# Spatial gating's four rounds, each moved one projection tile later

## What is computed

```
h = rms_norm(x, g);  z = h @ w_in
u_a, v_a = gelu(z[:, 0:512]), gelu(z[:, 512:1024])
q, k, v, f = the next 512, 512, 512 and 8 columns
vn = (v_a - mean) * rsqrt(var + eps) * ln_g          # per head of 64
mixed = w_s (masked, 128 x 128 per head) @ vn + b_s  # along a block of 128 positions
out_a = u_a * mixed
out_b = forgetting_attention(q, k, v, f)
x = x + concat(out_a, out_b) @ w_out
```

## Time and profile before

| | |
|---|---|
| median of 3 runs | 3130.44 us (3128.32 to 3130.82) |
| the profiled execution's own time | 3129.38 us |
| its span in the trace | 3127.3 us |
| TensorE busy with matmuls | 2930.7 us, 94% |
| VectorE busy | 1695.3 us, 54% |
| ScalarE busy | 984.3 us, 31% |
| GpSimd busy | 1028.5 us, 33% |
| mean DMA rate | 82 GB/s |

### The profile page before, as it was taken

How to read it: one execution, slowest core, us unless ns; L and a number is a source line. 1 busy time by engine, 2 the same in 40 slices (tenths; PEclk the granted TensorE clock), 3 DMA queues, 4 the chain that set the end, 5 groups by cost and what they waited for, 6 DMA issues and landing times. The chain is left out here.

```text
span 3127.3 us, 43902 instructions
## 1 busy us (share of the span) xinstructions
PE 2930.7 (94%) x16484; PEld 2419.3 (77%) x16484; DVE 1695.3 (54%) x2479; ACT 984.3 (31%) x1741; POOL 1028.5 (33%) x642
## 2 busy tenths in 40 slices
PE   7989899999999999899999989888889799999998
PEld 6768787778888888778878878878778577777776
DVE  5734353764554554555567348788842652067753
ACT  4021461311111111321111127677730201177731
POOL 2433313654445554422222212223243222211231
PEclk9989999999999999999999999999999899999998
DMA  5544521111111111023344321212011132432111
GB/s 182 182 137 136 136 62 47 54 54 47 47 40 47 47 54 40 20 102 113 125 168 148 114 104 43 102 52 94 18 40 37 54 132 76 127 99 51 28 41 68
DMA packets 214183, 255.72 MB, mean 82 GB/s; under 512 B 9401, under 2 KB 182782, under 8 KB 214030
## 3 DMA queue, kind: packets, MB, share of 16 engines
q1 hardware_dynamic: 198450, 190.20, 20.0%
q10 hardware_dynamic: 15584, 63.51, 5.1%
HBM read 188.08 MB, written 65.60 MB: 81 GB/s over the span
## 5 line engine op out<-in xcount | busy, mean ns | idle before, releaser
L1036 PE MATMUL ps<-hh,w_parts 128*128 128x512 f32 (+2 forms) x2560 | 999.8, 391 | 46.3 <-POOL w_parts L816 27.5
L1037 PE MATMUL ps<-hl,w_parts 128*128 128x512 f32 (+2 forms) x2560 | 984.3, 384 | 0.0
L1038 PE MATMUL ps<-hh,w_parts 128*128 128x512 f32 (+2 forms) x2560 | 981.4, 383 | 0.0
L1036 PEld LDWEIGHTS ps<-hh,w_parts 128*128 128x128 f32 x2560 | 488.9, 191 | 157.2 <-issue 37.4
L814 POOL TENSOR_TENSOR w_parts<-w_raw,zero 128x1024 fp32r<-128x1024 f32 x140 | 294.6, 2104 | 956.7 <-PE ps L1038 769.3
L1037 PEld LDWEIGHTS ps<-hl,w_parts 128*128 128x128 f32 x2560 | 490.6, 192 | 104.9 <-issue 5.7
L1038 PEld LDWEIGHTS ps<-hh,w_parts 128*128 128x128 f32 x2560 | 489.5, 191 | 99.9
L816 POOL TENSOR_TENSOR w_parts<-w_raw,w_parts 128x1024 fp32r<-128x1024 f32 x140 | 338.5, 2418 | 11.0
L1977 ACT ACTIVATE f_y<-f_z,convv 128x1024 f32<-128x1024 f32 x44 | 54.8, 1245 | 515.1 <-DVE f_z L2548 514.9
L2548 DVE TENSOR_TENSOR f_z<-ps,f_rs 128x1024 f32<-128x1024 f32 x44 | 53.8, 1223 | 182.9 <-PE ps L1038 182.7
L2750 DVE TENSOR_SCALAR_CACHE_REDUCE b_s<-ps 128x640 f32<-128x640 f32 (+1 forms) x128 | 99.9, 781 | 96.3 <-PE ps L1610 96.2
(11 more groups left out here) (355 smaller groups left out, 4799.3 us busy)
## 6 DMA issues: line engine op xcount, KB each, us to landing
w_mod_sb<-in_w_mod SPq DMA_DIRECT2D x16, 1536.0 KB, 6.9
w_raw<-in_w_up SPq DMA_DIRECT2D x44, 512.0 KB, 3.7
w_raw<-in_a_w_in SPq DMA_DIRECT2D x32, 512.0 KB, 4.4
d_raw<-in_w_down SPq DMA_DIRECT2D x22, 512.0 KB, 4.1
w_raw<-in_w_in SPq DMA_DIRECT2D x20, 512.0 KB, 5.4
za_parts<-z_hi ACTq DMA_DIRECT2D x16, 640.0 KB, 3.0
za_parts<-z_lo ACTq DMA_DIRECT2D x16, 640.0 KB, 4.0
d_even<-za_parts SPq DMA_DIRECT2D x16, 640.0 KB, 7.0
```

Of the source, the lines that this page charges most:

```text
L1036: pe.matmul(out_, w_hi, x_hi, start=start, stop=False)
L1037: pe.matmul(out_, w_hi, x_lo, start=False, stop=False)
L1038: return pe.matmul(out_, w_lo, x_hi, start=False, stop=stop)
```

## The change

On TensorE, turn of round j moves from behind tile (j, 0) to behind tile (j, 1), and mix from behind tile (j, 1) to behind tile (j + 1, 0). For round 3 the next tile is the first value tile, so `project_leaving` gets a call to make behind its first tile. The wait for the modulation's banks (`mod_kept`) moves along with the first turn. VectorE and ScalarE get the same order: the keep of the next pair's first tile now stands between normal and gate, the loop has three passes, and the fourth round stands behind it, on VectorE behind the scan of the forget gates, on ScalarE behind their store. SyncE's and GpSimd's programs are as before.

```
@@ project_leaving
-        def project_leaving(pe, name, tiles, segs):
-
-            with pe.Fori(0, tiles // 2 - 1) as i:
-                for s in range(2):
-                    project_tile(pe, name, i, s, segs)
+        def project_leaving(pe, name, tiles, segs, behind=None):
+
+            if behind is not None:
+                project_tile(pe, name, 0, 0, segs)
+                behind()
+                project_tile(pe, name, 0, 1, segs)
+            first = 0 if behind is None else 1
+            if tiles // 2 - 1 > first:
+                with pe.Fori(first, tiles // 2 - 1) as i:
+                    for s in range(2):
+                        project_tile(pe, name, i, s, segs)
@@ TensorE
                 if j == 0:
                     for s in range(2):
                         mod_sums(pe, 0, 3, s)
+                else:
+                    spatial_mix(j - 1)
+                project_tile(pe, "qk", j, 1, LATENT_SEGS)
+                if j == 0:
                     for s in range(2):
                         pe.wait_ge(mod_kept[s], 4 + 1)
                 spatial_turn(j)
-                project_tile(pe, "qk", j, 1, LATENT_SEGS)
-                spatial_mix(j)
-            project_leaving(pe, "vb", 4, LATENT_SEGS)
+            project_leaving(pe, "vb", 4, LATENT_SEGS, lambda: spatial_mix(3))
@@ ScalarE
-            with act.Fori(0, 4) as i:
-                qk_keep_high(i, 0)
+            qk_keep_high(0, 0)
+            with act.Fori(0, 3) as i:
+                qk_keep_high(i, 1)
                 spatial_spread(i)
-                qk_keep_high(i, 1)
+                qk_keep_high(i + 1, 0)
+            qk_keep_high(3, 1)
             act.wait_ge(f_scan, 5)
             for part in range(2):
                 act.dma_start(forget_rows[part], f_parts[:, part].bitcast(F32)).then_inc(f_stored, 16)
+            spatial_spread(3)
@@ VectorE
-            with dve.Fori(0, 4) as i:
-                qk_keep_low(i, 0)
+            qk_keep_low(0, 0)
+            with dve.Fori(0, 3) as i:
+                qk_keep_low(i, 1)
                 spatial_normal(i)
-                qk_keep_low(i, 1)
+                qk_keep_low(i + 1, 0)
                 spatial_gate(i)
...
+            qk_keep_low(3, 1)
+            spatial_normal(3)
+            spatial_gate(3)
```

## The result

The changed kernel took **3135.23 us** (median of 16 runs, 3130.81 to 3138.30). In the same series the kernel before took 3127.61 us (16 runs, 3123.61 to 3131.03). The ratio is 1.0022, with a 95% interval of 1.0016 to 1.0029: +6.9 us, between +5.0 and +9.1. The kernel before had been put at 3130.44 by three runs, and sixteen put it at 3127.61, 2.8 us lower. Of the difference, +4.5 was forecast and +6.9 measured. The two errors have opposite signs and nearly cancel.

The account below looks back on a forecast made before the run. TensorE is busy 94% of the span, but tile (1, 0) cannot start before its weights at 205.36 us. Terms -0.99 + 3.26 + 2.25 + 0 = +4.5 us on the 3130.44 median give 3134.9 us, range 3130.5 to 3139.0.

Parts of the forecast that it names:

- The removed wait: TensorE, round 0: the 6.4 us wait for `s_v` goes, 7.4 to 10.3 us waiting for pair 1's weights replaces it.
- Start of tile (1, 0): TensorE starts this tile when GpSimd's weight split ends, at 205.36 instead of 206.35 us: -0.99 us.
- Mix 0 on the path: Mix 0 leaves the place where late weights hid it and runs behind tile (1, 0): +3.26 us.
- The clock: Half speed after idle now falls on tile (1, 0): +2.25 us, bounds 1.56 to 2.92.
- The raw weights' landing: Load time of pair 1's weights, beside the stores of tile (0, 1): 0, bounds -1.35 to +2.0 us.
- Rival 1: Stores of tile (0, 1) delay pair 1's weights in full, 3.9 us more: +8.4 us, 3138.8 us; chance 0.15.
- Rounds 1 to 3: Same work reordered; mix still finds its inputs with a 1.3 us margin: cost 0.
- Rival 2: Rearranged loops miss the rounds' 1.3 us margin, three mixes wait 0.7 us each: +6.6 us, 3137.0 us; chance 0.10.
- The end of the stage: Attention's first loads go out about 5 us later, hidden under three value tiles: cost 0.
- The sum: All terms of the change together: +4.5 us, bounds +2.5 to +7.2.
- Rival 3: The wait ahead of tile (1, 0) simply goes, weights being there at 198 us: -8.0 us, 3122.4 us; chance 0.05.
- rival 4: Something else moves, by code placement or unrolled loops; no size given, spread evenly; chance 0.06.

Follow-up runs that it names:

- first early-weights run: Changed kernel with SyncE sending the weights of pair 1 ahead of round 0's fourteen loads: 3122.23 us, 0.9982 of the kernel before; run again 3121.66 us, 0.9983.
- mix_ahead: Changed kernel with mix 0 alone, and its gate 0, put back ahead of tile (1, 0), behind turn 0: 3135.57 us, 1.0023 of the kernel before.
- the two fills: Changed kernel with 32 or 46 unread matmuls behind turn 0, where TensorE waits for weights: 3132.57 us (1.0018) and 3133.63 us (1.0023 of the kernel before).
- r0_old: Changed kernel with round 0 alone put back to the old order on TensorE, VectorE and ScalarE: 3129.30 us, 1.0006 of the kernel before.
- early_before: Kernel before, with the weights of pair 1 sent ahead of round 0's loads: 3130.10 us, 1.0008 of the unedited kernel before.
- 46 fills: Changed kernel with 46 unread matmuls of 512 columns behind turn 0, where TensorE waits for weights: 3133.63 us, 1.0023 of the kernel before.

## Why the prediction held, and where it was off

The mechanism held: one wait was removed, another came in its place, and a mix and the slow start of the clock came onto the path. That the total came out within 0.3 us is partly luck, as said above, and 1.7 to 3.0 us of the measured change are not found in the stage that the prediction explains.

- **The removed wait** (7.4 to 10.3 us of idle forecast in place of 6.4): 10.40 and 10.47, just past the long end, because tile (0, 1) ran at full clock: 11.25 us from 181.15 to the turn. I had read the clock of 0.50 in the earlier trace rows as the one at which the tile would start. In that execution the clock had fallen in the sums already (2.96 us at a mean of 0.89, 2.73 when the kernel was run again); in both profiles of the change it had not (2.73 at 1.00). Where it did, in the first early-weights run and in mix_ahead, tile (0, 1) started at 0.50 as forecast. The prediction said that this hides in the wait; in the changed kernel the wait left room for it.
- **Start of tile (1, 0)** (-0.99): counted from the issue of the `s_w` load, 22.6 and 23.8 us in the two profiles of before, 21.9 and 22.0 now: -0.7 to -1.9.
- **Mix 0 on the path** (+3.26): 216.73 to 219.99 and 218.61 to 221.87, 3.26 both times, as forecast. Putting it back ahead of the tile does not save it, as mix_ahead shows.
- **The clock** (+2.25, bounds 1.56 to 2.92): tile (1, 0) took 216.73 - 204.05 = 12.68 and 218.61 - 204.54 = 14.07 us instead of 11.21: +1.47 and +2.86, mean 2.17. The lower of the two is 0.09 outside the bounds. With the wait filled to 1.3 us it is +0.06. The 2.25 was the middle of two cases and not derived; that the mean came so near it is luck.
- **The raw weights' landing** (0, bounds -1.35 to +2.0): 6.30 and 6.12 us from issue to split, before 6.05 and 7.20. The store of tile (0, 1) did go out at 196.54, three microseconds behind the weights, and did not hold them up. Rival 1 fell. The rule of the Trainium skill (page "DMA: Bandwidth & Descriptors", section "Issuing engines are not separate DMA queues"), that transfers of different issuers interleave, would at its dearest have added 2.0 us. No run shows such a delay: with the store behind the load, the changed kernel, the two fills and mix_ahead took 6.12 to 6.61 us, and without it the two profiles of before and r0_old took 6.05 to 7.20.
- **Rounds 1 to 3** (0, margin 1.3 us): normal 1 ended at 241.05 + 1.22 = 242.27 in the profile after, mix 1 began at 243.59: 1.32 us to spare. Rival 2 fell.
- **The end of the stage** (0): SyncE's `a_k` load went out at 305.33 instead of 302.54, under value tiles; the wait ahead of attention was 5.07 and 5.28 us (5.5 before). Counted from the sums that is 4.1 us later (126.77 instead of 122.64); forecast were about five. Attention's first matmul was to come near 342, that is 162.1 us behind the start of the sums; it came 160.9 and 162.6 behind it.
- **The sum** (+4.5): in the stage -1.4 (mean, counted from the start of the sums) + 3.26 + 2.17 = 4.0 by parts, 3.9 by its length. The mechanism and the terms hold. The range has a slip: its lower edge, 2.1 us below 3132.9, would be 3130.8 and not 3130.5.
- **Rival 3** (the wait simply goes, -8.0) was right about the price and wrong about the condition: once SyncE sends the weights early, it comes true. The argument against it, SyncE's unchanged order, was the one that counted.

**What stays open.** The timings say +6.9 (+5.0 to +9.1) and +5.6 us (+2.8 to +8.4); the stage holds 3.9. The forecast of 4.5 is below the first interval and inside the second. From attention's first matmul to the end, where both kernels run the same instructions, the profiles of before took 2789.9 and 2791.2 us, those of the change 2795.8 and 2796.4. But both profiled executions of the change were slower than their own medians, by 1.8 and 5.7 us. And that part took 2785.0 us in one execution of the early-weights kernel and 2792.2 in another; the other four profiles with the first turn moved lie between 2789.0 and 2793.8. So it can't be told whether the change costs 2 to 3 us there by some effect on what follows, or whether these are the spread of single executions.

Two rivals are not excluded. One is rival 4: early_before, which has the old order, also times 1.5 us above what its stage explains (+2.5 against 158.86 - 157.8 = +1.0), so a part may come with any edit. The other lies in the stage. GpSimd's second step begins only 0.4 us ahead of VectorE's last step of normal 0 in both profiles of the change. Where VectorE was no later, as with 46 fills, the weights were ready 1.1 us later, and some unprofiled executions may go that way. No run here tells.

The fastest version is the changed order with the weights of pair 1 sent ahead: 3122.2 and 3121.7 us, some 5.5 us (0.17%) below the kernel before and 12 to 13 below the changed one. That was run twice, and both intervals lie below 1.

## What to carry to other kernels

A wait that an engine makes can be cover for a later input: before filling it with other work, look at what that engine will want next, who sends it, and how many issues stand ahead of it in an in-order queue. Here fourteen loads in front of the weights, which went out 11.2 us behind the first of them, turned a good reordering into a loss, and moving the weights of that one pair ahead was worth 12 us. Work that lay free beside such a wait, here a mix and the slow start of the clock, comes onto the path when the wait moves.

## What the runs showed of the hardware

- **Idle and the clock.** 3.33 us of idle between matmuls was followed by a tile 2.7 us longer (202.34 to 216.28), 10.4 us by one 1.5 or 2.9 us longer; 1.29 us by one at full clock. So between 3.3 and 10.4 us of idle the price did not grow with the idle time.
- **The clock can fall during narrow matmuls.** The 24 one-column sums, with no idle ahead of them, are followed by tile (0, 1) in eight of the profiles. In six they took 2.73 us and turn 0 started 13.8 us behind their start. In the first early-weights run and in mix_ahead they took 3.05 and 3.04, and the turn started 16.96 and 15.42 us behind it. The first profile of the kernel before is a third case (2.96 us, mean clock 0.89), its second is not. What decides it is open.
- **A two-input step of VectorE and a GpSimd step shut each other out.** In the changed kernel the last step of normal 0 fell into GpSimd's split. VectorE's timeline:

```profile
202.10 2.97 DVE L2438 TENSOR_TENSOR s_ctr<-s_ctr,s_stat 128x1024 f32<-128x1024 f32 x1
...
241.05 1.22 DVE L2438 TENSOR_TENSOR s_ctr<-s_ctr,s_stat 128x1024 f32<-128x1024 f32 x1
```

The same instruction took 2.97 us (3.05 when the kernel was run again) beside GpSimd's step of 201.66 to 204.00, and 1.22 alone in round 1. It ended 1.07 us behind that step, about its own length, and GpSimd's next step, begun at 203.96, then took 2.87 instead of 1.89. With 46 fills VectorE's step began first (202.80 against 202.81) and it was GpSimd's that lost (3.45 instead of 2.34). Not every pair of steps does this: in the changed kernel a one-input reduction of VectorE, 200.19 to 201.41, ran beside GpSimd's step of 199.69 to 201.58, and both took their usual time (1.22 and 1.89). The Trainium skill's page "SBUF — State Buffer", section "SBUF: two separate sides", describes this as an exclusive lock on a port pair that the two share, where the loser fully blocks; the trace agrees with its 2.97 us. In the two profiles of the changed kernel it costs nothing, since mix 0 comes 12 us later; the prediction had not looked for it.
